# Nine small loads moved from SyncE's instruction stream to ScalarE's

## The chip, the cores and the metric

The kernel runs on one core of a Trainium2 chip. The metric is the device time of one execution in microseconds (us); before the change the median of three runs is 876.32 us. A trace of one further, profiled execution is read below. The core has five engines that follow instruction streams of their own: TensorE (PE in the rows; its weight loads are PEld), VectorE (DVE), ScalarE (ACT), GpSimd (POOL) and SyncE (SP), which in this kernel issues every load and store. The data of a load are moved by the core's 16 DMA engines. A load adds 16 to a semaphore when it has landed, and whoever needs the data waits for that.

## The reference, cut to what matters

One Conformer-convolution layer, then one latent attention layer, on 512 tokens of width 1024, all in float32:

```python
def conformer_conv_branch(h, w_in, b_in, conv_w, conv_b, norm_g, norm_b, w_out, b_out):
    proj = h @ w_in + b_in                       # 1024 -> 3 * 2048
    val, glu_gate, z = jnp.split(proj, 3, axis=-1)
    u = val * jax.nn.sigmoid(glu_gate)
    u = causal_depthwise_conv(u, conv_w) + conv_b    # 31 taps per channel
    u = jax.nn.silu(layer_norm(u, norm_g, norm_b)) * jax.nn.silu(z)
    return u @ w_out + b_out

h = layer_norm(alpha * x + conformer_conv_branch(x, ...))
k_nope, k_rope, v = shared_latent_kv(h, ...)         # rotary tables from `positions`
h = layer_norm(alpha * h + mla_branch(h, k_nope, k_rope, v, ...))
```

## The kernel before, in words

Every float32 product is computed as three faster ones: each operand is split into a rounded part (`_hi`) and the rest (`_lo`), and TensorE computes lo*hi + hi*lo + hi*hi. ScalarE makes the `_hi` of each weight chunk `c` (line 710), GpSimd its `_lo` (line 566), from a raw tile of 512 KB that SyncE loaded (line 402); there are two raw tiles and four split ones.

The start, which the change touches, goes so. SyncE issues the loads of the four row blocks of x (`x_in`, 512 KB each, line 412), and after the second and the fourth of them one of the first two weight chunks (`w_raw`, line 402). Then come the nine small loads (lines 416 to 424): the convolution taps `taps_raw` (31 partitions of 2048 words), six groups of vectors into `vec_raw` (102 partitions in all, of 128 words), the rotary frequencies `freq`, and `pos_int`, the positions copied to 128 partitions. All nine count on one semaphore, `small_landed`. After them SyncE loads the chunks c = 2, 3 and so on, each when its raw tile has been split (line 110 is the helper's wait).

TensorE turns x block by block (32 transposes, line 1427, eight for each row block); ScalarE copies each group of four out of PSUM as `xt_hi` (line 771), and VectorE makes `xt_lo` (line 1032). ScalarE makes `w_hi` of chunk 0 after the fourth of these eight copies and of chunk 1 after the eighth. With all of `xt_lo` there, TensorE computes chunk 0 (24 products of 128x512, line 1416, wait in `columns`). Behind chunk 0, and only there, it waits for `small_landed`, turns the taps (16 transposes, line 1434) and the vectors (one, line 1437), and goes on with chunk 1, 2 and the rest. ScalarE copies the turned taps and vectors (lines 778 and 780) before it splits chunk 2 and moves the first result out of PSUM with its bias. VectorE waits for `small_landed` as well: it computes the angles of the rotary tables (lines 1045 to 1059), and then begins the convolution (lines 1088 and 1093).

The order on each engine is the order of the code; no planner is involved. From chunk 1 on TensorE has work to the end, with short waits only.

Of the kernel before, what the change touches and what calls it, by code (L numbers as in the profile page):

```python
# [32 lines left out]
P = 128  # L33
# [3 lines left out]
SEQ = 512  # L37
# [18 lines left out]
CT = CONV_WIDTH // P  # L56
RT = SEQ // P
KQ = Q_RANK // P
KV = KV_RANK // P
# [30 lines left out]
V_BIN = 0  # L90
V_CONVB = V_BIN + 3 * CT
V_NG = V_CONVB + CT
V_NB = V_NG + CT
V_KVG = V_NB + CT
V_QG = V_KVG + KV
# [17 lines left out]
def trunk_kernel(nc, x, positions, ln_g, ln_b, a_w_in, a_b_in, a_conv_w, a_conv_b, a_norm_g,  # L113
# [14 lines left out]
    with ExitStack() as ctx:  # L128
        def sem(name):
            return ctx.enter_context(nc.semaphore(name))  # L130
# [10 lines left out]
        def at(name, base, offset_words, shape, dtype=F32):  # L141
            return nc.alloc_sbuf_tensor_at(name, shape, dtype, offset=base + 4 * offset_words)

        def own(name, shape, dtype=F32):
            words = 1
            for n in shape[1:]:
                words *= n
            return at(name, region(words), 0, shape, dtype)
# [20 lines left out]
        freq = own("freq", [P, 2])  # L169
# [29 lines left out]
        taps_raw = at("taps_raw", reg_acc, 0, [TAPS, CONV_WIDTH])  # L199
        vec_raw = at("vec_raw", reg_acc, 4 * TILE, [V_ALL, P])  # L200
        pos_int = at("pos_int", reg_acc, 5 * TILE, [P, SEQ], I32)
# [90 lines left out]
        small_landed = sem("small_landed")  # L292
# [56 lines left out]
        def added_before(n):  # L349

            return sum(1 for _, k in shared_taps[:n] if k > 0)
# [43 lines left out]
        def _(sp):  # L395
# [5 lines left out]
            def load_columns(slot, source, column):  # L401
                sp.dma_start(w_raw[slot][:].rearrange("p (k m) -> p k m", m=P),
                             source[:, :, bass.ds(column, P)]).then_inc(w_landed[slot], 16)

            def load_value_gate(j, first=0):
                for s in range(first, ROUND):
                    for w in range(2):
                        raw_free(2 * ROUND * j + 2 * s + w)
                        load_columns(w, w_in_a, w * CONV_WIDTH + (ROUND * j + s) * P)

            for r in range(RT):
                sp.dma_start(x_in[:, r, :], x_rows[:, r, :]).then_inc(x_landed[r], 16)  # L412
                if r % 2 == 1:
                    w = r // 2
                    load_columns(w, w_in_a, w * CONV_WIDTH)
            sp.dma_start(taps_raw[:], a_conv_w[0]).then_inc(small_landed, 16)  # L416
            for row, vector, n in ((V_BIN, a_b_in, 3 * CT), (V_CONVB, a_conv_b, CT),
                                   (V_NG, a_norm_g, CT), (V_NB, a_norm_b, CT), (V_QG, b_q_norm_g, KQ)):
                sp.dma_start(vec_raw[row:row + n, :], vector.rearrange("a (n p) -> (a n) p", p=P)  # L419
                             ).then_inc(small_landed, 16)  # L420
            sp.dma_start(vec_raw[V_KVG:V_KVG + KV, :], kv_norm_g.rearrange("(n p) -> n p", p=P)
                         ).then_inc(small_landed, 16)
            sp.dma_start(freq[:], rope_freq).then_inc(small_landed, 16)
            sp.dma_start(pos_int[:], positions.broadcast_to([P, SEQ])).then_inc(small_landed, 16)
            load_value_gate(0, 1)
            with sp.Fori(1, ROUNDS) as j:
                load_value_gate(j)
# [278 lines left out]
        def _(act):  # L706
            def split_hi(c, raw, slot, landed):
                act.wait_ge(w_landed[raw], landed)
                wait(act, w_used, c - SLOTS + 1)
                nc.scalar.activation(w_hi[slot][:], w_raw[raw][:], ACT.Copy).then_inc(w_hi_ready, 1)  # L710
# [54 lines left out]
                                     bias=vec[:, V_CONVB + t:V_CONVB + t + 1]).then_inc(pe_conv_kept, 1)  # L765


            for q in range(2 * RT):
                r, half = q // 2, q % 2
                act.wait_ge(x_turned, q + 1)  # L770
                nc.scalar.activation(xt_hi[:, 4 * half:4 * half + 4, r * P:(r + 1) * P],
                                     bank[q % 4][:].rearrange("p (k n) -> p k n", k=4), ACT.Copy
                                     ).then_inc(xt_hi_ready, 1)
                if q % 4 == 3:
                    split_hi(q // 4, q // 4, q // 4, 16)
# [197 lines left out]
            def transposed_hi(h):  # L973
                for g, (from_bank, group, _) in enumerate(turn_groups):
                    act.wait_ge(prob_turned, 3 * h + g + 1)
                    for b, first in group:
                        nc.scalar.activation(pt_hi[:, 0:b + 1, b * P:(b + 1) * P],
                                             bank[from_bank][:, first:first + (b + 1) * P].rearrange(
                                                 "p (k n) -> p k n", k=b + 1), ACT.Copy).then_inc(pt_hi_ready, 1)
# [773 lines left out]
```

## Time and profile before

| | |
|---|---|
| median of 3 runs | 876.32 us (876.02 to 878.18) |
| profiled execution | 877.75 us |
| its span, first to last instruction | 876.0 us |
| mean granted clock of TensorE | 0.995 of full |
| TensorE busy | 851.5 us, 97% |
| VectorE, GpSimd, ScalarE busy | 601.8, 471.8, 398.2 us |
| DMA queue q1 | 78.44 MB, 30.2% of 16 engines |

The profiled execution took 1.75 us more than its span, for what lies around it. Times in rows are in us from the start of the span, those marked ns excepted. A row of the timeline gives the start of a piece, its length, engine, line, operation, tiles and count, and in brackets the idle time of the engine before it with what ended it. In the timeline matmuls are pipelined: one that lasts 0.40 us can start 0.23 us after the one before. DMA share is the mean busy share of the 16 DMA engines, so that one engine at work alone shows as 0.06. SPq is SyncE's own time to issue a load.

### The profile page before, as it was taken

To read this page: it belongs to the slowest core of one execution; us is meant where nothing else is said; L and a number is where in the kernel's file an instruction comes from. 1 tells how busy PE (TensorE), PEld (TensorE's weight loads), DVE (VectorE), ACT (ScalarE), POOL (GpSimd) and SP (SyncE) were. 2 spreads that over 40 slices of the span, in tenths; PEclk is the share of its full clock that TensorE was granted. 3 is DMA by queue.
4 is the path that set the end of the run, shared out by engine and by line. 5 is a ranking of instruction groups with operands and counts; after the bars stand their busy time and mean duration, and the time that the engine had idled before them with its cause. 6 is when DMAs were issued, how large, how long until landed. Compare 5 with 4: busy or idle time off the path is not lost.

```text
span 876.0 us, 11846 instructions
## 1 busy us (share of the span) xinstructions
PE 851.5 (97%) x4083; PEld 708.4 (81%) x4083; DVE 601.8 (69%) x1089; ACT 398.2 (45%) x690; POOL 471.8 (54%) x260
## 2 busy tenths in 40 slices
PE   6999999999999999999999999999999999989996
PEld 5788888888888788788898788788888898878885
DVE  2899999999999749321723380157977878787207
ACT  3555444444564467431332443255555546554110
POOL 3577988896996572493454456142432433136431
PEclk9899999999999999999999999999999999999999
DMA  6232333330024323453143324323123230224212
GB/s 214 75 96 74 97 96 96 96 97 25 1 73 125 109 80 103 142 186 98 49 121 109 97 72 133 84 73 84 42 56 84 72 84 15 70 97 145 97 48 97
DMA packets 111399, 78.99 MB, mean 90 GB/s; under 512 B 14071, under 2 KB 98141, under 8 KB 111325
## 3 DMA queue, kind: packets, MB, share of 16 engines
q1 hardware_dynamic: 111356, 78.44, 30.2%
q8 instruction: 24, 0.39, 0.2%
q14 instruction: 19, 0.16, 0.1%
HBM read 71.87 MB, written 2.10 MB: 84 GB/s over the span
## 4 chain that ended last, share of the span: by engine, by line
PE 95%; DMA 2%; DVE 1%; SPq 1%; issue 1%; ACT 1%; DVEq 0%; ACTq 0%
PE bank L1416 89%; PE bank L1679 2%; DMA pos_int<-in_positions_dram 2%; PE bank L1668 1%; PE bank L1669 1%; PE bank L1554 0%; SPq L419 0%; DVE fg_lo L1400 0%; SPq L412 0%; PE bank L1434 0%; PE bank L1606 0%; PE bank L1495 0%; DVE pt_lo L1355 0%; SPq L416 0%; ACT prob L970 0%
## 5 line engine op out<-in xcount | busy, mean ns | idle before, releaser
L566 POOL TENSOR_TENSOR w_lo<-w_raw,w_hi 128x1024 fp32r<-128x1024 f32 x103 | 253.6, 2472 | 189.3 <-ACT w_hi L710 163.4
L1093 DVE SCALAR_TENSOR_TENSOR bank<-u,conv_w,bank 128x512 f32<-128x512 f32 x348 | 233.8, 759 | 0.9
L710 ACT ACTIVATE w_hi<-w_raw 128x1024 fp32r<-128x1024 f32 x103 | 107.0, 1054 | 117.6 <-PE bank L1416 66.8
L1416 PE MATMUL bank<-xt_hi,w_lo 128*128 128x512 f32 x384 | 153.6, 400 | 1.4 <-DVE xt_lo L1032 1.4
L1416 PE MATMUL bank<-xt_lo,w_hi 128*128 128x512 f32 x384 | 152.4, 397 | 0.0
L1416 PE MATMUL bank<-xt_hi,w_hi 128*128 128x512 f32 x384 | 152.3, 397 | 0.0
L1416 PEld LDWEIGHTS bank<-xt_hi,w_lo 128*128 128x128 f32 x384 | 73.1, 190 | 19.3 <-DVE xt_lo L1032 1.8
L1416 PEld LDWEIGHTS bank<-xt_lo,w_hi 128*128 128x128 f32 x384 | 72.9, 190 | 17.2 <-issue 0.5
L1416 PEld LDWEIGHTS bank<-xt_hi,w_hi 128*128 128x128 f32 x384 | 72.9, 190 | 17.2
L593 POOL TENSOR_TENSOR acc<-acc,tap_product 128x512 f32<-128x512 f32 x60 | 77.9, 1299 | 8.5 <-ACT tap_product L744 1.6
L664 POOL TENSOR_TENSOR bundle_lo<-bundle_raw,bundle_hi 128x1024 fp32r<-128x1024 f32 (+1 forms) x16 | 47.0, 2957 | 63.1 <-ACT bundle_hi L905 63.1
L1416 PE MATMUL bank<-ht_hi,w_lo 128*128 128x512 f32 (+1 forms) x208 | 76.4, 367 | 0.0
L1416 PE MATMUL bank<-ht_lo,w_hi 128*128 128x512 f32 (+1 forms) x208 | 75.8, 365 | 0.0
L1416 PE MATMUL bank<-ht_hi,w_hi 128*128 128x512 f32 (+1 forms) x208 | 75.8, 365 | 0.0
L1209 DVE SCALAR_TENSOR_TENSOR bank<-res,bank 128x512 f32<-128x512 f32 x16 | 11.0, 690 | 93.7 <-PE bank L1416 63.3
L744 ACT ACTIVATE tap_product<-u,conv_w 128x512 f32<-128x512 f32 x60 | 41.8, 719 | 33.5 <-POOL acc L593 33.4
L970 ACT ACTIVATE prob<-prob,neg_top 128x512 f32<-128x512 f32 (+1 forms) x64 | 35.5, 556 | 42.3 <-DVE neg_top L1314 42.3
L1416 PE MATMUL bank<-w_hi,g_lo 128*128 128x512 f32 x128 | 51.1, 399 | 1.6 <-issue 1.6
L1416 PE MATMUL bank<-w_hi,fg_lo 128*128 128x512 f32 x128 | 50.9, 398 | 1.2 <-DVE fg_lo L1400 1.2
L1416 PE MATMUL bank<-w_hi,fg_hi 128*128 128x512 f32 x128 | 50.6, 395 | 0.0
L1416 PE MATMUL bank<-w_hi,g_hi 128*128 128x512 f32 x128 | 50.6, 395 | 0.0
L1416 PE MATMUL bank<-w_lo,fg_hi 128*128 128x512 f32 x128 | 50.3, 393 | 0.0
(196 smaller groups left out, 1795.1 us busy)
## 6 DMA issues: line engine op xcount, KB each, us to landing
w_raw<-in_a_w_in_dram SPq DMA_DIRECT2D x48, 512.0 KB, 3.7
w_raw<-in_b_w_in_dram SPq DMA_DIRECT2D x20, 512.0 KB, 3.6
w_raw<-in_a_w_out_dram SPq DMA_DIRECT2D x16, 512.0 KB, 4.1
w_raw<-in_b_w_out_dram SPq DMA_DIRECT2D x16, 512.0 KB, 3.5
bundle_raw<-in_b_w_uq_dram SPq DMA_DIRECT2D x16, 256.0 KB, 3.8
x_in<-in_x_dram SPq DMA_DIRECT2D x4, 512.0 KB, 5.8
res<-in_x_dram SPq DMA_DIRECT2D x4, 512.0 KB, 5.0
bundle_raw<-in_kv_w_uk_dram SPq DMA_DIRECT2D x8, 256.0 KB, 2.9
```

What stands on the lines that cost most here:

```text
L566: nc.gpsimd.tensor_tensor(w_lo[slot][:], w_raw[raw][:], w_hi[slot][:].bitcast(F32), ALU.subtract).then_inc(w_lo_ready, 1)
L593: nc.gpsimd.tensor_tensor(acc[:, t, :], acc[:, t, :], tap_product[n % 2][:], ALU.add).then_inc(product_added, 1)
L664: nc.gpsimd.tensor_tensor(bundle_lo[slot][part][:], bundle_raw[:, lo:hi], bundle_hi[slot][part][:].bitcast(F32), ALU.subtract).then_inc(bu ...
L710: nc.scalar.activation(w_hi[slot][:], w_raw[raw][:], ACT.Copy).then_inc(w_hi_ready, 1)
L744: nc.scalar.activation(tap_product[n % 2][:], u[:, t, k:k + SEQ], ACT.Copy, scale=tap).then_inc(product_ready, 1)
L970: nc.scalar.activation(block_, block_, ACT.Exp, bias=neg_top[:, b:b + 1], scale=SM_SCALE, accum_out=denom[:, b:b + 1]).then_inc(exp_done, 1)
L1093: nc.vector.scalar_tensor_tensor(out=bank[CONV_BANK[slot]][:] if k < TAPS - 1 else acc[:, t, :], in0=u[:, t, k:k + SEQ], scalar=conv_w[:, ...
L1209: nc.vector.scalar_tensor_tensor(out=total[:], in0=rows_half, scalar=scale, in1=total[:], op0=ALU.mult, op1=ALU.add).then_inc(y_step, 1)
L1416: last = nc.tensor.matmul(out_ap, a, b, start=(start and n == 0 and m == 0), stop=(stop and n == len(parts) - 1 and m == 2))
L1668: nc.tensor.matmul(bank[score_bank[i]][:, 0:n], stack[:, cut], kr_lo[:, 0:n], start=False, stop=False)
L1669: nc.tensor.matmul(bank[score_bank[i]][:, 0:n], stack[:, cut], kr_hi[:, 0:n], start=False, stop=True).then_inc(scores_done, 1)
L1679: last = nc.tensor.transpose(bank[to_bank][:, first + k * P:first + (k + 1) * P], prob[:, (prob_at[b] + k) * P:(prob_at[b] + k + 1) * P], ...
```

## The change

The nine small loads are issued by ScalarE in place of SyncE. Their sources, destinations, sizes and semaphore are the same, and so is their order among themselves. On ScalarE they stand ahead of everything else; what SyncE issued behind them now follows directly on the first two weight chunks.

```diff
@@ SyncE @@
                     load_columns(w, w_in_a, w * CONV_WIDTH)
-            sp.dma_start(taps_raw[:], a_conv_w[0]).then_inc(small_landed, 16)
-            for row, vector, n in ((V_BIN, a_b_in, 3 * CT), (V_CONVB, a_conv_b, CT),
-                                   (V_NG, a_norm_g, CT), (V_NB, a_norm_b, CT), (V_QG, b_q_norm_g, KQ)):
-                sp.dma_start(vec_raw[row:row + n, :], vector.rearrange("a (n p) -> (a n) p", p=P)
-                             ).then_inc(small_landed, 16)
-            sp.dma_start(vec_raw[V_KVG:V_KVG + KV, :], kv_norm_g.rearrange("(n p) -> n p", p=P)
-                         ).then_inc(small_landed, 16)
-            sp.dma_start(freq[:], rope_freq).then_inc(small_landed, 16)
-            sp.dma_start(pos_int[:], positions.broadcast_to([P, SEQ])).then_inc(small_landed, 16)
             load_value_gate(0, 1)
@@ ScalarE @@
+            act.dma_start(taps_raw[:], a_conv_w[0]).then_inc(small_landed, 16)
+            for row, vector, n in ((V_BIN, a_b_in, 3 * CT), (V_CONVB, a_conv_b, CT),
+                                   (V_NG, a_norm_g, CT), (V_NB, a_norm_b, CT), (V_QG, b_q_norm_g, KQ)):
+                act.dma_start(vec_raw[row:row + n, :], vector.rearrange("a (n p) -> (a n) p", p=P)
+                             ).then_inc(small_landed, 16)
+            act.dma_start(vec_raw[V_KVG:V_KVG + KV, :], kv_norm_g.rearrange("(n p) -> n p", p=P)
+                         ).then_inc(small_landed, 16)
+            act.dma_start(freq[:], rope_freq).then_inc(small_landed, 16)
+            act.dma_start(pos_int[:], positions.broadcast_to([P, SEQ])).then_inc(small_landed, 16)
             for q in range(2 * RT):
```

On SyncE, at the start of its stream, between the first two weight chunks and chunks 2 and 3:

```order
 L412 DMA x_in<-in_x_dram 128x1024 x2
 L402 DMA w_raw_71<-in_a_w_in_dram 128x8x128
-L416 DMA taps_raw<-in_a_conv_w_dram 31x2048
-L419 DMA vec_raw<-in_a_b_in_dram 48x128
-L419 DMA vec_raw<-in_a_conv_b_dram 16x128
-L419 DMA vec_raw<-in_a_norm_g_dram 16x128
-L419 DMA vec_raw<-in_a_norm_b_dram 16x128
-L419 DMA vec_raw<-in_b_q_norm_g_dram 4x128
-L421 DMA vec_raw<-in_kv_norm_g_dram 2x128
-L423 DMA freq<-in_rope_freq_dram 128x2
-L424 DMA pos_int<-in_positions_dram 128x512
 L402 DMA w_raw_70<-in_a_w_in_dram 128x8x128
```

The nine rows are gone there, and chunk 2 stands right behind chunk 1. On ScalarE, at the start of its stream, ahead of the table load and the first copy of turned x:

```order
+L759 DMA taps_raw<-in_a_conv_w_dram 31x2048
+L762 DMA vec_raw<-in_a_b_in_dram 48x128
+L762 DMA vec_raw<-in_a_conv_b_dram 16x128
+L762 DMA vec_raw<-in_a_norm_g_dram 16x128
+L762 DMA vec_raw<-in_a_norm_b_dram 16x128
+L762 DMA vec_raw<-in_b_q_norm_g_dram 4x128
+L764 DMA vec_raw<-in_kv_norm_g_dram 2x128
+L766 DMA freq<-in_rope_freq_dram 128x2
+L767 DMA pos_int<-in_positions_dram 128x512
 L771 ACT_TABLE_LOAD
```

The same nine now come first, the taps at their head, and the load of the activation table comes behind all of them. The instructions of TensorE, VectorE and GpSimd are the same, in the same order.

## Rows read from the trace of the kernel before

**Rows 1.** Part 4 of the page: the chain that ended last, by engine.

```profile
PE 95%; DMA 2%; DVE 1%; SPq 1%; issue 1%; ACT 1%; DVEq 0%; ACTq 0%
```

**Rows 2.** The chain that ended last, first 60 us: start, length, what.

```profile
4.25 1.53 SPq L416
...
9.84 13.83 DMA pos_int<-in_positions_dram
...
23.72 1.85 PE bank L1434 x16
25.57 0.36 PE bank L1437
25.93 34.07 PE bank L1416 x137
```

**Rows 3.** Timeline of TensorE, 0 to 34 us.

```profile
4.18 3.65 PE L1427 MATMUL bank<-ident,x_in 128*128 128x128 f32 x16 [4.18 <-DMA x_in<-in_x_dram]
9.67 3.68 PE L1427 MATMUL bank<-ident,x_in 128*128 128x128 f32 x16 [1.84 <-DMA x_in<-in_x_dram]
14.76 0.50 PE L1416 MATMUL bank<-xt_hi,w_lo 128*128 128x512 f32 x1 [1.41 <-DVE xt_lo L1032]
...
20.21 0.40 PE L1416 MATMUL bank<-xt_hi,w_hi 128*128 128x512 f32 x1
23.72 1.85 PE L1434 MATMUL bank<-ident,taps_raw 31*128 31x31 f32 x16 [3.11 <-DMA pos_int<-in_positions_dram]
...
25.63 0.77 PE L1416 MATMUL bank<-xt_hi,w_lo 128*128 128x512 f32 x1
...
33.58 0.40 PE L1416 MATMUL bank<-xt_hi,w_lo 128*128 128x512 f32 x1
```

**Rows 4.** Stretches: engines' busy time and count, granted clock, DMA share, GB/s.

```profile
7.00:8.00 1.00, 0.82 (x4) 0.42 (x2) 0.84 (x2) 0.73 (x2) 0.00 (x0) 1.00 1.02 384
...
16.00:17.00 1.00, 1.00 (x6) 0.80 (x5) 0.00 (x0) 0.00 (x0) 1.00 (x1) 1.00 0.06 25
17.00:18.00 1.00, 1.00 (x6) 0.82 (x5) 0.00 (x0) 0.00 (x0) 0.40 (x1) 1.00 0.06 25
...
```

**Rows 5.** DMA packets from 17 to 18 us.

```profile
DMA packets 3, 0.02 MB, mean 25 GB/s; under 512 B 0, under 2 KB 0, under 8 KB 0
```

**Rows 6.** DMA issues of the first 60 us: count, KB, us to landing.

```profile
pos_int<-in_positions_dram SPq DMA_DIRECT2D x1, 256.0 KB
taps_raw<-in_a_conv_w_dram SPq DMA_DIRECT2D x1, 248.0 KB
```

**Rows 7.** The same for the issue at 2.75 us (fourth block of x) alone.

```profile
x_in<-in_x_dram SPq DMA_DIRECT2D x1, 512.0 KB, 8.1
```

**Rows 8.** The same for the issue at 11.97 us (chunk 2) alone.

```profile
w_raw<-in_a_w_in_dram SPq DMA_DIRECT2D x1, 512.0 KB, 12.6
```

**Rows 9.** Timeline of SyncE, 0 to 45 us.

```profile
2.12 1.59 SPq L412 DMA_DIRECT2D x_in<-in_x_dram  x2
3.76 0.44 SPq L402 DMA_DIRECT2D w_raw<-in_a_w_in_dram  x1
4.25 1.53 SPq L416 DMA_DIRECT2D taps_raw<-in_a_conv_w_dram  x1
...
9.84 0.43 SPq L424 DMA_DIRECT2D pos_int<-in_positions_dram  x1
11.97 31.56 SPq L402 DMA_DIRECT2D w_raw<-in_a_w_in_dram  x6
```

**Rows 10.** Timeline of ScalarE, 0 to 45 us.

```profile
0.75 1.28 ACT L771 ACT_TABLE_LOAD   x1 [0.75 <-PEq L1740]
5.30 0.60 ACT L771 ACTIVATE xt_hi<-bank 128x512 fp32r<-128x512 f32 x1 [3.27 <-PE bank L1427]
...
10.82 0.60 ACT L771 ACTIVATE xt_hi<-bank 128x512 fp32r<-128x512 f32 x1 [1.38 <-PE bank L1427]
```

**Rows 11.** Stretches, columns as in rows 4: at half clock and at full clock.

```profile
23.90:30.30 6.40, 6.40 (x28) 5.37 (x28) 6.13 (x8) 4.59 (x6) 2.79 (x2) 0.50 0.03 9
...
37.00:60.00 23.00, 23.00 (x100) 18.65 (x100) 22.54 (x34) 13.52 (x27) 15.86 (x8) 1.00 0.32 92
```

**Rows 12.** Timeline of GpSimd, 0 to 45 us.

```profile
9.53 2.36 POOL L566 TENSOR_TENSOR w_lo<-w_raw,w_hi 128x1024 fp32r<-128x1024 f32 x1 [6.17 <-ACT w_hi L710]
15.00 2.39 POOL L566 TENSOR_TENSOR w_lo<-w_raw,w_hi 128x1024 fp32r<-128x1024 f32 x1 [3.12 <-ACT w_hi L710]
27.51 5.01 POOL L566 TENSOR_TENSOR w_lo<-w_raw,w_hi 128x1024 fp32r<-128x1024 f32 x2 [10.11 <-ACT w_hi L710]
```

**Rows 13.** Timeline of VectorE, 0 to 302 us.

```profile
23.70 0.43 DVE L1045 CAST pos<-pos_int 128x512 f32<-128x512 int32 x1 [8.99 <-DMA pos_int<-in_positions_dram]
...
36.33 0.81 DVE L1088 TENSOR_SCALAR bank<-u,conv_w,vec 128x512 f32<-128x512 f32 x1 [0.20 <-POOL u L571]
...
295.01 0.69 DVE L1078 TENSOR_TENSOR csum<-bank,acc 128x512 f32<-128x512 f32 x1
301.00 1.29 DVE L1146 SCALAR_TENSOR_TENSOR acc<-bank,acc 128x512 f32<-128x512 f32 x2 [5.30 <-PE bank L1488]
```

## The prediction

> **What bounds the kernel now.** I read the chain of waits first. TensorE is 95% of it [rows 1], and from 25.93 us on the chain is the products of line 1416 almost without a break; the only DMA piece of weight is the landing of `pos_int` at 23.67 us [rows 2]. So what happens before 25.63 us, where chunk 1 begins, moves the end one for one, and nothing else in the change can. Then the timeline of TensorE shows what that start is made of [rows 3]: a wait for the first block of x to 4.18, for the third to 9.67, chunk 0 from 14.76 to about 20.6, an idle time of 3.11 us for `small_landed`, 1.9 us of small transposes, and chunk 1 from 25.63 to 33.58. Chunk 1 takes 7.95 us where 24 products at full speed take 5.6: the granted clock is 0.50 from 23.9 to 30.3, the lower of TensorE's two levels (1.2 against 2.4 GHz), after the idle time had brought it down, and 28 matmuls start in 6.4 us there against 100 in 23 us at full clock [rows 11]. The stall thus costs 3.1 us itself and some 2.35 us in chunk 1, besides some 0.7 us in the transposes.
>
> Third, why do the small loads land so late? They were all issued by 10.27 us [rows 9]. From 15.6 to 18.9 us the DMA share is 0.06, one engine of 16, at 25 GB/s, where up to 11 us it had been about 1.0 at up to 384 GB/s [rows 4]. In one such microsecond three packets pass, 0.02 MB, none under 8 KB [rows 5]. The only load with pieces of 8 KB is `taps_raw`, 31 partitions of 8 KB. So the taps, 248 KB [rows 6], go through a single DMA engine: 254 kB at 25 GB/s are 10.2 us. Chunk 2, issued at 11.97 behind them, needs 12.6 us to land [rows 8]: each load has a share on this engine and must wait for the taps there. I call it the slow engine. It is busy without a pause: x, w and x until about 11 us, the taps until about 21, then the vectors and positions.
>
> **The change part by part.** *SyncE's nine issues go.* They took it from 4.25 to 10.27 us [rows 9], but chunk 2 could not be issued before chunk 0 had been split, at 9.53 + 2.36 = 11.89 us [rows 12], and was issued at 11.97; so this is worth nothing.
>
> *ScalarE's nine issues come.* The price on ScalarE has no row. SyncE's 6.0 us for the same nine is one end; nine times the 0.44 us of a plain issue [rows 9], 4.0 us, the other. They begin at 0.75, and the table load of 1.28 us [rows 10] now follows: ScalarE is ready between 6.0 and 8.1 us, where its first copy stood at 5.30. By itself that delays the first four copies by 0.7 to 2.8 us; the idle time before the fifth copy (1.38 us [rows 10]) absorbs part, so 0 to 1.5 us reach the first product. In my forecast x is later than that and hides it: 0.
>
> *The small loads start 3.5 us earlier, beside x instead of behind it.* This is the main term. On the slow engine x (four shares of 32 KB), chunk 0 and chunk 1 (32 KB each) and the taps (254 kB) need the same time as before, in whatever order; what changes is who is first. Before, x's fourth block was issued at 2.75 and landed 8.1 us later, at 10.85 [rows 7], ahead of all the taps. Now the taps stand at the head of a second queue from 0.75 us on. If the slow engine takes pieces from the two queues in turn, then by the time it has taken the 40 pieces of 4 KB that x and chunk 0 make up (or more, counting chunk 0's pieces of 512 bytes singly), all 31 pieces of 8 KB are through. The fourth block then lands 10.2 us later: 21.05 us. A block of x is of use only when all 16 engines have delivered, so 15 idle engines don't help. Bounds for this term: 0 (SyncE's queue always first) and 11 us (taps, vectors and positions all ahead).
>
> The Trainium skill, DMA: Bandwidth & Descriptors, section "Issuing engines are not separate DMA queues", says that loads started by several engines run on the same 16 DMA engines, interleaved, and that only the issue time is saved. Its section "Queues, rings and completion order" adds that each DMA engine takes packets from its queues in turn. No row of before can show this, since one queue carries all its loads; by that rule the term is the full 10.2 us, and if one queue always had precedence it would be 0.
>
> *The sum, from x to the end of chunk 1.* The first product stood at 14.76, 3.9 us behind the landing of the fourth block; now it stands at 21.05 + 3.9 = 25.0 us. Chunk 0 takes 5.8 us (14.76 to 20.6): 30.8. `small_landed` is long there (about 20 us), so the stall of 3.1 us is gone. The 17 small transposes took 1.9 us at half clock; between 1.0 and 1.9, I take 1.2: 32.0. Chunk 1 at full clock 5.6: 37.6. Now the clock. Before it fell once, after the 3.1 us of idleness, and came back 6.6 us after work resumed. Now TensorE waits longer and earlier: from about 12 us, with the second block turned, to about 20, when the third lands. The clock falls there; if it comes back 6.6 us after the transposes resume, chunk 0 loses half a microsecond, and if only 6.6 us after the first product, 3.0 us. I take 1.8. End of chunk 1: 39.4 us against 33.58, that is 5.8 us later.
>
> *What else could be late then.* GpSimd has `w_lo` of chunk 1 ready 2.7 us behind the first product (15.00 + 2.39) [rows 12], hence by about 28 us, and it is wanted at 32. `w_lo` of chunk 2 follows the small transposes by 4.4 us as before (half of the 5.01 us behind 27.51), and chunk 1 takes 5.6 us at full clock: 1.1 us to spare. VectorE starts its tables when small loads and `xt_lo` are there, about 25 us instead of 23.70, needs 12.6 us, and starts the convolution with the first `u`, 5.8 us later than 36.33; it has its sum at 295.7 and then idles for 5.30 us until TensorE has used it, and both shift alike [rows 13]. So nothing takes anything back: 877.75 + 5.8 = 883.55 us for the profiled execution, whose time lay 1.43 us above the median, and 882.1 us for the median.
>
> **The rivals.** *A, the forecast:* the taps delay x: 882.1 us, by its own unknowns (the clock 0.5 to 3.0 us, transposes 1.0 to 1.9, the delay 9.6 to 11) 880 to 885.5.
>
> *B, equal bytes:* the slow engine shares by bytes, not by pieces. x and chunk 0 are 164 kB there, 6.6 us at 25 GB/s; at half rate the fourth block is 6.6 us late instead of 10.2. That gives 3.6 us less: +2.2, 878.5 us.
>
> *C, faster:* x keeps its landing at 10.85 while the taps arrive in its shadow. The place is the slow engine between 2 and 11 us, and it decides whether this engine has room to spare when fed from two queues. For it: only the 31 taps of 8 KB limp, and a queue of large serial pieces might leave capacity unused. Against it: the 25 GB/s of one engine times 16 is 400, about the 384 of all engines together [rows 4], so the engine seems full with either kind. With room, the first product stands at 14.76 to 16.3 (ScalarE's issues), chunk 0 ends at 21.4, transposes 1.2, chunk 1 5.6 without a dip: 28.2 or so against 33.58, -5.4: 870.9 us.
>
> *D, nothing:* SyncE's queue is served first, so that the taps run from 11 us on as before and everything lands where it landed; ScalarE's 0 to 1.5 us vanish in the stall. 876.3 us. Partly so if ScalarE's issues are slow to take effect.
>
> *E, worse:* descriptors of the two issuers block each other, so that x slows on all engines and not only on one; 3 to 6 us above A, 885 to 888.
>
> **How the numbers follow.** A 0.63, B 0.11, C 0.12, D 0.08, E 0.06. The time is A's, 882.1. The range reaches from 872 (it leaves out most of C) to 886.5 (it leaves out half of E and A's tail); A's own range stands above. A measurement of this kernel tells about 0.3% (2.6 us) from nothing, so slower means above 878.9 and faster below 873.7: slower is A, E and some of B, 0.71; same is D, most of B, 0.17; faster is C, 0.12.
>
> **What would show it.** In the profile after: the fourth block of x lands about 21 us, with the DMA share low (0.1) while TensorE waits for x between 12 and 20; the first product of line 1416 at about 25; no wait for `small_landed` at line 1434; a granted clock of 0.50 somewhere between 15 and 31; chunk 2's first product at about 39; and the same durations from there on. The prediction is wrong in its main step if the fourth block lands before 15 us; then the time is at or below 876. It is wrong in its second if the clock stays full (3 us less) or if a wait appears at chunk 2 or 3.

## The result, and the profile after

The changed kernel takes 885.51 us in the median of five runs (883.84 to 885.97), against 878.18 us (876.02 to 879.53) for five runs of the kernel before: 7.3 us more, a ratio of 1.0082 with an interval of 1.0064 to 1.0099. In a second measurement of the same two it was 1.0074 (1.0056 to 1.0093). It is slower, as forecast. The forecast of 882.1 us was a median of 876.32 plus 5.8 us. Of the 3.4 us by which the time lies above it, 1.9 are that base, which came out at 878.18 beside the changed kernel, and 1.5 are the change itself.

The timeline of TensorE at the start, of the kernel after (the same view as [rows 3]):

```profile
8.88 1.94 PE L1427 MATMUL bank<-ident,x_in 128*128 128x128 f32 x8 [8.88 <-DMA x_in<-in_x_dram]
13.11 1.97 PE L1427 MATMUL bank<-ident,x_in 128*128 128x128 f32 x8 [2.29 <-DMA x_in<-in_x_dram]
21.11 3.67 PE L1427 MATMUL bank<-ident,x_in 128*128 128x128 f32 x16 [6.04 <-DMA x_in<-in_x_dram]
26.20 0.80 PE L1416 MATMUL bank<-xt_hi,w_lo 128*128 128x512 f32 x1 [1.41 <-DVE xt_lo L1032]
...
26.79 0.63 PE L1416 MATMUL bank<-xt_lo,w_hi 128*128 128x512 f32 x1
27.22 0.63 PE L1416 MATMUL bank<-xt_hi,w_hi 128*128 128x512 f32 x1
...
30.20 0.57 PE L1416 MATMUL bank<-xt_hi,w_lo 128*128 128x512 f32 x1
...
33.95 1.18 PE L1434 MATMUL bank<-ident,taps_raw 31*128 31x31 f32 x16
...
35.14 0.48 PE L1416 MATMUL bank<-xt_hi,w_lo 128*128 128x512 f32 x1
...
40.80 0.39 PE L1416 MATMUL bank<-xt_hi,w_lo 128*128 128x512 f32 x1
```

The idle time for the small loads is gone: line 1434 starts without a wait. In its place stand longer waits for x: 8.88, 2.29 and 6.04 us, where there were 4.18 and 1.84. The third block used to be there at 9.67 us and is now there at 21.11, so chunk 0 begins at 26.20 instead of 14.76. Until 30.2 us its matmuls start 0.43 us apart, then 0.23. Chunk 1 takes 5.66 us instead of 7.95, and chunk 2 begins at 40.80 instead of 33.58: 7.2 us later. The span grew by 7.7 us (883.7 against 876.0), so all but 0.5 us of the loss is there by chunk 2. The sum, from the rows: third block +11.44, chunk 0 +1.9, stall -3.11, small transposes -0.7, chunk 1 -2.3, together +7.2.

Where the data were is seen in the DMA views of the kernel after. First the loads of the third and of the fourth block of x, with their us from issue to landing (7.5 and 8.1 before), and SyncE's timeline of the two issues, with the fourth block's issue by itself in the last line:

```profile
x_in<-in_x_dram SPq DMA_DIRECT2D x1, 512.0 KB, 18.9
x_in<-in_x_dram SPq DMA_DIRECT2D x1, 512.0 KB, 13.5
```

```profile
2.12 9.74 SPq L412 DMA_DIRECT2D x_in<-in_x_dram  x2
...
8.78 3.09 SPq L412 DMA_DIRECT2D x_in<-in_x_dram  x1
```

The fourth block was issued at 8.78 and landed at 22.3, where it had landed at 10.85: 11.4 us later, like the third.

Then stretches of it (columns as in [rows 4]), and the DMA packets and queues from 8.3 to 9.3 and from 18.3 to 19.0 us. q1 is SyncE's queue, q10 the new one of ScalarE; their columns are pieces, MB and share:

```profile
8.00:9.00 1.00, 0.12 (x1) 0.15 (x2) 0.00 (x0) 0.00 (x0) 0.00 (x0) 1.00 0.05 20
...
10.00:11.00 1.00, 0.82 (x4) 0.42 (x2) 0.37 (x1) 0.74 (x2) 0.00 (x0) 1.00 1.03 397
...
13.00:14.00 1.00, 0.89 (x4) 0.90 (x5) 0.00 (x0) 0.00 (x0) 0.00 (x0) 1.00 0.98 349
...
18.00:19.00 1.00, 0.00 (x0) 0.00 (x0) 0.00 (x0) 0.00 (x0) 0.00 (x0) 1.00 0.07 24
```

```profile
DMA packets 4, 0.02 MB, mean 25 GB/s; under 512 B 0, under 2 KB 0, under 8 KB 2
...
q10 hardware_dynamic: 2, 0.02, 3.9%
q1 hardware_dynamic: 2, 0.01, 2.0%
```

```profile
q10 hardware_dynamic: 7, 0.01, 4.6%
q1 hardware_dynamic: 8, 0.00, 1.9%
```

At 8 us and again from 18 us to the landing, one engine of 16 works and 15 wait, now with x behind it. In between the other engines do work, in bursts: SyncE's issue of the third block lasted from 2.12 to 8.74 us, that of the fourth to 11.87, and chunk 1 came behind them, so that the other engines, too, moved the later blocks of x late, at 9 to 14 us instead of by 11. That cost nothing of its own, for the share of the slow engine landed last.

The counts show the turns. From 8.3 to 9.3 us this engine moved two pieces of 8 KB of the taps and two of 4 KB of x; from 18.3 to 19.0 it moved seven of ScalarE's queue (those of the positions, 2 KB) and eight of SyncE's (those of chunk 0, 512 bytes): one for one, whatever their size. For the first microseconds, in which all engines are busy, the counts don't separate the slow engine, and the turns alone don't give the first block's time: eight turns of 0.33 us (10.2 us for 31 pieces) behind the 4.18 of before are 6.8 us, an estimate, and it was there at 8.88. ScalarE's issues are no bottleneck:

```profile
0.74 0.52 ACTq L759 DMA_DIRECT2D taps_raw<-in_a_conv_w_dram  x1
...
4.50 0.45 ACTq L767 DMA_DIRECT2D pos_int<-in_positions_dram  x1
4.98 1.28 ACT L771 ACT_TABLE_LOAD   x1 [4.98 <-issue]
10.00 0.60 ACT L771 ACTIVATE xt_hi<-bank 128x512 fp32r<-128x512 f32 x1 [3.74 <-PE bank L1427]
```

The nine take 4.2 us and ScalarE is ready at 6.26; then it waits 3.74 us for TensorE, which waits for x.

### The profile page after: what moved, and what is told of

The parts are those of the page before. It is cut to its first block, busy times and chain, and to the rows that moved or that the text cites. A ratio compares the mean times of both kernels' runs of the same rounds, so it can differ in the third digit from the quotient of the medians.

```text
span 883.7 us, 11846 instructions
## 1 busy us (share of the span) xinstructions
PE 850.9 (96%) x4083; PEld 707.1 (80%) x4083; DVE 599.9 (68%) x1089; ACT 397.9 (45%) x690; POOL 471.3 (53%) x260
## 4 chain that ended last, share of the span: by engine, by line
PE 93%; DMA 3%; DVE 2%; issue 1%; ACT 1%; SPq 0%; DVEq 0%; ACTq 0%
PE bank L1416 88%; DMA x_in<-in_x_dram 2%; PE bank L1679 2%; PE bank L1668 1%; PE bank L1669 1%; PE bank L1427 0%; PE bank L1554 0%; DMA qr_stack<-qr_lo 0%; DVE pt_lo L1355 0%; DVE fg_lo L1400 0%; ACT prob L970 0%; DVE prob L1325 0%; PE bank L1606 0%; PE bank L1495 0%; DVE q_lo L1345 0%
## 5 line engine op out<-in xcount | busy, mean ns | idle before, releaser
L1416 PE MATMUL bank<-w_lo,g_hi 128*128 128x512 f32 x128 | 50.3, 393 | 0.0
```

The lines of the kernel that those rows point to most:

```text
L1416: last = nc.tensor.matmul(out_ap, a, b, start=(start and n == 0 and m == 0), stop=(stop and n == len(parts) - 1 and m == 2))
```

## The experiments

Each time stands beside runs of the kernel before on the same chip: in the first four experiments its median was 877.59, in the next two 878.10, in the last three 878.26 us. Behind a median stands its ratio to the kernel before, with its interval. Each timeline is of one profiled execution. The diffs of e1, e2 and e5 are in outline, against the changed kernel; where the number of small loads changes, so does the count that `small_landed` is compared with.

**Taps alone on ScalarE (e1).** The other eight loads are back on SyncE, behind chunk 1's load.

```diff
 SyncE    load_columns(w, w_in_a, w * CONV_WIDTH)
+         (the eight loads other than the taps)
 ScalarE  taps_raw
-         (the eight loads other than the taps)
```

> Only the taps' load is issued by ScalarE; the other eight go back to SyncE, behind the first two weight chunks. Theory T (the taps' 31 pieces of 8 KB all pass through one DMA engine, which takes pieces of SyncE's and ScalarE's queues in turn, so that the taps delay x): the third block of x lands about 20 us (9.6 before, 21.07 after the change; 1 us less than after, since vectors and positions are no longer ahead), the first product is at about 25, and the time is 6 to 7 us above before. Rival Q (a second queue in use, or ScalarE's nine issues ahead of its copies, is what costs): with one issue instead of nine the delay is mostly gone, under 2 us above before.

883.76 us, 1.0064 (1.0048 to 1.008): 6.2 us above before. TensorE's timeline:

```profile
19.82 3.68 PE L1427 MATMUL bank<-ident,x_in 128*128 128x128 f32 x16 [5.25 <-DMA x_in<-in_x_dram]
24.91 0.79 PE L1416 MATMUL bank<-xt_hi,w_lo 128*128 128x512 f32 x1 [1.41 <-DVE xt_lo L1032]
```

The third block is there at 19.82, 1.3 us earlier than after the change, the first product at 24.91. Theory T holds; the number of ScalarE's issues is not the cost. SyncE's issues of the third and fourth block take 9.18 us together here, so that goes with the taps as well.

**Eight on ScalarE, taps on SyncE (e2).**

```diff
 SyncE    load_columns(w, w_in_a, w * CONV_WIDTH)
+         taps_raw
 ScalarE
-         taps_raw
          (the eight others)
```

> The other way round: eight loads on ScalarE, the taps on SyncE as before. T: x lands at most 1.5 us later than before (0.36 MB of vectors and positions over 16 engines, 0.9 us), the first product at 15 to 16.3; the taps still end near 21 us, so the wait for the small loads shrinks from 3.1 to about 1 us; the time is between 4 us below and 0.5 us above before, by whether the clock still falls in that shorter idle time. Q: eight of nine issues and the second queue are still there, so x stays at 18 us or later and the time is 5 us or more above before.

878.01 us, 1.0009 (1.0000 to 1.0019): no change that can be told. TensorE's timeline:

```profile
9.12 1.09 PE L1427 MATMUL bank<-ident,x_in 128*128 128x128 f32 x8 [1.65 <-DMA x_in<-in_x_dram]
...
13.95 0.79 PE L1416 MATMUL bank<-xt_hi,w_lo 128*128 128x512 f32 x1 [1.41 <-DVE xt_lo L1032]
23.48 1.56 PE L1434 MATMUL bank<-ident,taps_raw 31*128 31x31 f32 x16 [2.21 <-DMA pos_int<-in_positions_dram]
```

A second queue with eight of the nine loads costs x nothing (9.12 for the third block against 9.67). The small loads are complete at 23.48, hardly before the 23.72 of [rows 3]. I had expected the taps to end near 21 us and about 1 us of idleness; it was 2.21. The packets from 22.0 to 22.7 us in this kernel are still the taps:

```profile
DMA packets 3, 0.02 MB, mean 35 GB/s; under 512 B 0, under 2 KB 0, under 8 KB 0
```

The last load was the taps and not `pos_int`, as the row has it. The vectors and positions now pass the slow engine ahead of the taps instead of behind them, so that all nine are there at the same time as before. Chunk 0 takes 7.3 us here (from 13.95 to 21.27, where the wait begins) against 5.8, and uses up what its earlier start had won.

**The kernel before with the taps in two loads, 16 and 15 partitions (e3).**

```diff
-            sp.dma_start(taps_raw[:], a_conv_w[0]).then_inc(small_landed, 16)
+            for lo, hi in ((0, 16), (16, TAPS)):
+                sp.dma_start(taps_raw[lo:hi, :], a_conv_w[0][lo:hi, :]).then_inc(small_landed, 16)
```

> The kernel before, all loads on SyncE, but the taps in two loads of 16 and 15 partitions instead of one of 31. T: a load of 31 partitions sits on one DMA engine because 31 is prime; 16 and 15 spread over 16 and 15 engines. The 248 KB then pass in under 1 us, the small loads land about 15 us, inside chunk 0 (14.76 to 20.6). The idle time of 3.1 us goes, and with it the fall of the clock (2.35 us in chunk 1, 0.7 in the transposes): 6 us below before, about 870. Rival S (the number of partitions does not matter, the 8 KB pieces are what goes over one engine, or the row length): nothing changes, 3.1 us of idleness stay.

870.88 us, 0.9931 (0.9916 to 0.9946): 6.7 us faster than before, the best version tried. TensorE's timeline, then the DMA packets from 10 to 11 us:

```profile
8.90 2.33 PE L1428 MATMUL bank<-ident,x_in 128*128 128x128 f32 x16 [1.14 <-DMA x_in<-in_x_dram]
12.80 0.50 PE L1417 MATMUL bank<-xt_hi,w_lo 128*128 128x512 f32 x1 [1.57 <-DVE xt_lo L1033]
18.57 1.17 PE L1435 MATMUL bank<-ident,taps_raw 31*128 31x31 f32 x16
19.76 0.48 PE L1417 MATMUL bank<-xt_hi,w_lo 128*128 128x512 f32 x1
25.42 0.39 PE L1417 MATMUL bank<-xt_hi,w_lo 128*128 128x512 f32 x1
```

```profile
DMA packets 414, 0.37 MB, mean 374 GB/s; under 512 B 29, under 2 KB 391, under 8 KB 391
```

In this microsecond 23 pieces of 8 KB pass (414 less 391), where three passed in [rows 5]: the taps are spread.

No wait stands behind chunk 0, and chunk 1 takes 5.66 us: the stall and its dip of the clock were worth 3.11 + 0.7 + 2.3 = 6.1 us. In this execution the third block was also there 0.8 us earlier and its 16 transposes ran in 2.33 us instead of 3.68, so that the first product came 1.96 us earlier. That part goes with the execution: e7 below, with the same loads, has 9.67, 3.48 and 14.56 us, close to before.

**The same split in the changed kernel (e4).** `act.dma_start` in the place of `sp.dma_start` in the diff of e3, all small loads on ScalarE.

> The changed kernel (all small loads on ScalarE) with the taps in two loads of 16 and 15 partitions. T: the small loads are 0.6 MB over 16 engines and delay x by 1.5 us; third block at about 11, first product at about 16.3, no wait behind chunk 0, no fall of the clock behind it: 4 to 5 us below before and about 1.5 us above the kernel with the taps split on SyncE. Q: the second queue costs in itself, x at 18 us or later, slower than before. S: as the changed kernel, 7 us above before.

875.04 us, 0.9969 (0.9955 to 0.9984): 2.6 us below before, where I had expected 4 to 5, and 4.2 above e3. TensorE's timeline:

```profile
11.57 3.68 PE L1428 MATMUL bank<-ident,x_in 128*128 128x128 f32 x16 [0.91 <-DMA x_in<-in_x_dram]
16.66 0.79 PE L1417 MATMUL bank<-xt_hi,w_lo 128*128 128x512 f32 x1 [1.41 <-DVE xt_lo L1033]
23.99 1.18 PE L1435 MATMUL bank<-ident,taps_raw 31*128 31x31 f32 x16
```

With the taps spread, moving the nine loads to ScalarE still costs 1.9 us of landing (11.57 against 9.67 before); chunk 0, with matmuls 0.43 us apart at first, takes the rest of what was missing (7.3 us instead of 5.8). So most of the delay is in one load's shape: 11.4 us with it, 1.9 without. But moving the loads isn't free even then: e4 is 4.2 us above e3. In the two profiled executions 2.7 us of that are landing (11.57 against 8.90), and the rest is the clock (transposes 3.68 against 2.33 us, chunk 0 7.3 against 5.8), which may differ between executions as well.

**Half of the taps ahead (e5).**

```diff
+ ScalarE  taps_raw[:, 0:D_MODEL], ahead of the eight
+ SyncE    taps_raw[:, D_MODEL:CONV_WIDTH], behind chunk 1's load
```

> The changed kernel with the taps in two loads by columns: the first half of each row (31 pieces of 4 KB) by ScalarE as in the change, the second half by SyncE behind the first two weight chunks. T: only 5.1 us of taps and 0.9 us of the rest pass ahead of x on the slow engine, so the third block of x lands 6 us later than before, about 15.6, and the first product is at about 20.7; the second half follows chunk 1 and lands about 23, inside chunk 0, so no wait there. From 5.1 of the 10.3 us taken away and a clock that is low for part of chunk 0: 0 to 3 us above before. Rival Q (cost of the second queue as such): the third block stays at about 20 us, 6 us above before.

879.26 us, 1.0007 (0.9996 to 1.0017): 1.2 us above before by the medians, inside the expected 0 to 3, and by the interval no change that can be told. TensorE's timeline:

```profile
15.08 3.30 PE L1428 MATMUL bank<-ident,x_in 128*128 128x128 f32 x16 [3.56 <-DMA x_in<-in_x_dram]
19.91 0.50 PE L1417 MATMUL bank<-xt_hi,w_lo 128*128 128x512 f32 x1 [1.52 <-DVE xt_lo L1033]
25.68 1.18 PE L1435 MATMUL bank<-ident,taps_raw 31*128 31x31 f32 x16
```

The delay of the third block is 5.4 us with half of the taps ahead, 11.4 with all, and there is no wait behind chunk 0. There are still 31 pieces ahead, each half as long: half the bytes, half the delay.

**The same bytes in pieces of 2 KB (e6).**

```diff
-            act.dma_start(taps_raw[:], a_conv_w[0]).then_inc(small_landed, 16)
+            for at_column in range(0, CONV_WIDTH, BANK):
+                act.dma_start(taps_raw[:, at_column:at_column + BANK], a_conv_w[0][:, at_column:at_column + BANK]
+                             ).then_inc(small_landed, 16)
```

> The changed kernel with the taps in four loads by columns, all on ScalarE ahead of the rest: the same bytes on the same engine, but 124 pieces of 2 KB instead of 31 of 8 KB. T with turns by piece: until x's second block is through, only 16 turns of 0.084 us go to the taps instead of 16 of 0.309; the first block of x lands about 4.7 instead of 8.7 us, the second about 6.7 instead of 13.0; chunk 0's 64 pieces of 512 bytes then let 64 taps pieces pass, so the third block lands about 17.5 instead of 21. Time 3 us below the changed kernel, 3 to 5 above before. Rival B (the engine shares by bytes): pieces of another size change nothing, first block at 8.7 us, time as the changed kernel.

880.35 us, 1.003 (1.0019 to 1.004): 2.3 us above before by the medians, somewhat less than the 3 to 5 expected. TensorE's timeline:

```profile
6.01 1.94 PE L1429 MATMUL bank<-ident,x_in 128*128 128x128 f32 x8 [6.01 <-DMA x_in<-in_x_dram]
8.25 1.97 PE L1429 MATMUL bank<-ident,x_in 128*128 128x128 f32 x8 [0.30 <-DMA x_in<-in_x_dram]
16.71 3.96 PE L1429 MATMUL bank<-ident,x_in 128*128 128x128 f32 x16 [6.49 <-DMA x_in<-in_x_dram]
22.08 0.80 PE L1418 MATMUL bank<-xt_hi,w_lo 128*128 128x512 f32 x1 [1.41 <-DVE xt_lo L1034]
```

The load's bytes are the same, the engine is the same, and yet the first block is ready at 6.01 instead of 8.88 us, the second by 8.25 instead of 13.11, the third at 16.71 instead of 21.11. Sharing by bytes (rival B of the prediction) falls; the engine takes turns by piece. The sizes were not exact: 4.7, 6.7 and 17.5 us had been expected.

**The clock at the start (e7 to e9).** In e8 TensorE turns the identity while it waits for x, 28, 10 and 36 times; e9 is the changed kernel again; e7 is e3 with eleven such transposes ahead of the first block.

```diff
             for r in range(RT):
+                for _ in range((28, 10, 36, 0)[r]):
+                    nc.tensor.transpose(bank[7][:, 0:P], ident[:], ident[:])
                 pe.wait_ge(x_landed[r], 16)
```

> The changed kernel, with 28, 10 and 36 extra transposes of the identity on TensorE while it waits for the first, second and third block of x (their result is not used). The term for the clock is tried alone: without a wait that leaves TensorE idle, the clock is full when the third block lands. Theory T with the clock term of 1.9 us: 16 transposes take 2.3 instead of 3.7 us and nine gaps of chunk 0 0.23 instead of 0.43, together 3.1 us below the changed kernel, some 4 above before. The third block still lands at about 21 us. Rival (the clock has no share in the loss of the changed kernel, which is landing time alone): within 0.5 us of the changed kernel, 7 above before.

> The changed kernel again, as it is, beside the two others on the same chip: 7 us above before (1.0082 measured), the measure for the kernel with extra transposes.

> The kernel before with the taps in two loads of 16 and 15 partitions, all on SyncE, and eleven extra transposes of the identity on TensorE while it waits for the first block of x (their result is not used). Theory W: the spread of about 3 us between executions of one kernel comes from when TensorE's clock rises at the start; with work from 1.5 us on it rises before the transposes of x in every execution, 16 of which take 2.3 us at full clock and 3.7 at half. Time 0.5 to 2 us below the kernel with the taps split alone, and less spread. Rival N (the clock's rise at the start hangs on nothing that the kernel does in the first 4 us): same time, same spread, within 0.5 us.

e8 took 882.8 us, 1.0057 (1.0039 to 1.0075), e9 884.24 us, 1.0074 (1.0056 to 1.0093): 1.4 us less, with intervals that overlap, so neither the 3 us of T nor the nothing of its rival. TensorE's timeline of e8, then of e9:

```profile
21.07 2.31 PE L1429 MATMUL bank<-ident,x_in 128*128 128x128 f32 x16 [1.32 <-DMA x_in<-in_x_dram]
24.95 0.50 PE L1416 MATMUL bank<-xt_hi,w_lo 128*128 128x512 f32 x1 [1.57 <-DVE xt_lo L1032]
30.73 1.18 PE L1436 MATMUL bank<-ident,taps_raw 31*128 31x31 f32 x16
```

```profile
20.87 3.54 PE L1427 MATMUL bank<-ident,x_in 128*128 128x128 f32 x16 [5.94 <-DMA x_in<-in_x_dram]
25.82 0.50 PE L1416 MATMUL bank<-xt_hi,w_lo 128*128 128x512 f32 x1 [1.41 <-DVE xt_lo L1032]
...
31.59 1.18 PE L1434 MATMUL bank<-ident,taps_raw 31*128 31x31 f32 x16
```

In e8 the third block lands when it did (21.07), the transposes take 2.31 us, and chunk 0 runs at full clock. But in e9, the unchanged kernel, chunk 0 ran at full clock too (5.8 us), where in the first profile of the same kernel it had taken 7.75. The moment at which the clock rises thus differs between executions of one kernel by enough to be worth 1.9 us. Without this term that execution took 883.47 us, still 5.7 us above the profiled execution before (877.75): the loss is there without it, and smaller.

e7 took 873.7 us, 0.9951 (0.9934 to 0.9968), no better than e3, and its nine runs spread from 871.39 to 877.93, where e3's six went from 869.72 to 873.48. Theory W falls: work from 1.5 us on did not settle the clock. Rival N, which wanted the time within 0.5 us, isn't borne out either. Its trace has the transposes of the third and fourth block at 3.48 us, the first product at 14.56, close to before, and no wait behind chunk 0:

```profile
9.67 3.48 PE L1430 MATMUL bank<-ident,x_in 128*128 128x128 f32 x16 [2.32 <-DMA x_in<-in_x_dram]
14.56 0.50 PE L1417 MATMUL bank<-xt_hi,w_lo 128*128 128x512 f32 x1 [1.41 <-DVE xt_lo L1033]
20.33 1.18 PE L1437 MATMUL bank<-ident,taps_raw 31*128 31x31 f32 x16
```

## Why the prediction was right

*The main term.* The forecast let the taps pass ahead of x on one DMA engine. e1 and e2 show that the taps alone do it, e5 that half of them gives half the delay, e3 and e4 that it hangs on the load's 31 partitions, since 16 + 15 takes 9.5 of the 11.4 us away, and the rows of both queues with e6 that the turns go by piece. Its size was low: 10.2 us forecast, 11.4 measured. What was left out of it is the eight other loads, which also went ahead of the third block: e1, without them there, has it 1.3 us earlier, at 19.82 - 9.67 = 10.15 us of delay, which is the 10.2 of the taps. The upper bound of 11 us counted them, and was itself 0.4 us too low. The step from the fourth block to the first product held: 22.3 + 3.9 = 26.2 us. Chunk 2 came at 40.80 instead of 39.4, and 1.2 of these 1.4 us are the delay. With the base 1.9 us higher as well, the time lies 1.0 us inside the upper end of the range and at the very edge of A's own.

*The stall and chunk 1.* Gone as forecast: -3.11, -0.7 and -2.3 us. e3 shows them alone, 6.1 us by its rows.

*The clock.* I took 1.8 us for chunk 0 and the first profile has 1.9, but the reason given, a fall of a full clock during the wait from 12 to 20 us, is wrong: the transposes of the very first block take as long (1.94 us for eight) as those of the third (3.67 for 16), against 2.31 for 16 at full clock in e8, so the clock was low before that wait. It was low at the start of the kernel before, too: 3.65 and 3.68 us for 16 transposes [rows 3]. "Before it fell once" overlooks that it had to rise first. After the change the full clock came at about 30.5 us, 9.4 us after the third block's transposes began and 4.3 after the first product, between the two moments that I had weighed. And e9 had no such cost. The size was right for that one execution by luck, and the term is no steady cost of the change.

*ScalarE's issues.* 4.2 us, near the lower of the two ends, and hidden by x's delay, as forecast. *Nothing gives anything back:* the 7.2 us at chunk 2 are 7.7 us in the span.

*The signs.* The third and fourth block at 21.11 and 22.3, the first product at 26.20, no wait at line 1434 and none at chunk 2 came as named. Two did not: between 12 and 20 us the DMA share was low from 17 us on alone (0.14 there, 0.98 from 13 to 14), and the granted clock of 0.50 stands nowhere in the column, only in the distance between starts.

*The rivals.* B falls by e6 and by the counts from 8.3 to 9.3 us, where the taps got two thirds of the bytes. C, D: x was not spared. E happened in part: SyncE's third and fourth issue took 9.74 us together instead of 1.59, so that the other engines moved x late as well, and chunk 1, the load behind, was in time all the same. It took none of the time that I had given it, since the slow engine was later still.

## What to carry to other kernels

Before a load gets a queue of its own, look whether it spreads over all DMA engines: a stretch with a DMA share of 1/16 while everybody waits is the sign that it does not, and then a second queue only lets it in ahead of the loads that count. Split the partitions first (here 31 into 16 and 15, 6.7 us for one line), and leave it behind the urgent loads on the same queue (e3 against e4, 4.2 us). No run tried the taps on ScalarE's queue at a later place, behind the issues of x. A load that is needed late gains nothing from an early start, and the urgent block that it delays is complete only when its slowest engine has delivered.

## What the runs showed of the hardware

- A load of 31 partitions went through one DMA engine, 31 pieces of 8 KB at about 25 GB/s; loads of 16 and 15 did not. The Trainium skill, DMA: Bandwidth & Descriptors, section "Why a DMA increments its semaphore by 16 and not by 1", has the rule that the number of engines is the largest up to 16 that divides the slowest dimension, hence one for 31. The trace agrees: three pieces of 8 KB passed in a microsecond with 31 partitions [rows 5], 23 with 16 and 15 (e3).
- Two queues on one engine took turns piece by piece: two against two in 1.0 us, 8 KB against 4 KB, and seven against eight in 0.7 us, 2 KB against 512 bytes. The queue with the smaller pieces got fewer bytes: with 2 KB in place of 8 KB the first block of x was ready 2.9 us earlier.
- SyncE's issues lasted longer the more the other queue had put on the slow engine. Its third and fourth issue took 9.74 us together after the change, 9.18 with the taps alone (e1), 5.06 with half of them (e5), 3.30 with pieces of 2 KB (e6), 1.58 with the taps spread (e4) and 1.59 before. That an issue waits for room at its slowest engine is my inference from these.
- The granted clock in the rows is to be read with care at the start. The profile after gives 1.00 for the first of these stretches, in which three matmuls are under way, and 1.00 for the second, in which six are:

```profile
27.00:28.00 1.00, 1.00 (x3) 0.78 (x3) 1.00 (x1) 0.00 (x0) 1.00 (x1) 1.00 0.00 0
32.00:33.00 1.00, 1.00 (x6) 0.82 (x5) 0.93 (x3) 0.00 (x0) 0.00 (x0) 1.00 0.05 15
```

The distance between starts tells the clock where the column doesn't: it is 0.43 us in the first stretch and 0.23 in the second, and in the kernel before it was 0.43 where the column gave 0.50 (26.62 and 27.05 us).
